# Hybrid attention layer on one core: the first norm's gain moved from x into the input weights, x loaded in half tiles

## The chip, the cores and the metric

The kernel runs on one core of a Trainium2 chip. The metric is the device time of one execution in microseconds; of several executions the median is given.

## The reference, cut to what matters

One decoder layer in float32 over 512 positions of width 1024. x is normalised and multiplied by a gain per feature, and one input projection of 1976 columns feeds both attention groups; output projection, second norm and a squared-ReLU MLP follow.

```python
def rms_norm(x, g):
    y = xf * lax.rsqrt(jnp.mean(xf * xf, axis=-1, keepdims=True) + EPS)
    return (y * g.astype(jnp.float32)).astype(x.dtype)

h = rms_norm(x, ln1_g) @ w_in      # columns: cq 384, ckv 256 + kr 32, nq 512, nsa k/v 768, gates 24
```

Since the gain stands on the contracted feature, (x * g) @ W equals x @ (g * W). The kernel leaves the factor per position, rsqrt of the mean square, until the results are read out of PSUM.

## The kernel before, in words

**Products in three parts.** Each float32 operand is split into a rounded high part (fp32r, written by ACT, the scalar engine) and the low remainder (written by DVE, the vector engine). PE (the tensor engine) forms a product as high times high, high times low and low times high (`three`, L2105 to L2110).

**Pieces of weights.** `PIECES` lists the weights in the order in which they are used, as pieces of up to 128x1024 values. Pieces 0 to 3 are block "cq" (768 columns: two feature chunks of 384), 4 to 7 "ckv" (576), then come uq, nq, ukv, nkv, cmp and others. Of the input projection's blocks (`IN_BLOCKS`) there are 20 pieces, four of each block. SP, the queue of SyncE, loads piece n into one of three `raw` buffers (L727), and must first wait for the low half of piece n-3 (`raw_free`). `split_hi` (ACT, L955 to L966) and `split_lo` (DVE, L1383 to L1394) turn it into the two halves in a ring of five. In between SP issues what `TURNED_AT`, `ROWS_AT` and `COPIES` name for a piece: the transposed tiles of x ahead of pieces 0, 2 and 3, the four row tiles of x ahead of piece 4, `gain_c` after piece 4, the constants after piece 6.

**x.** It is loaded twice: by rows (`x`, for the squares in `ln1_square`, L986) and features-first, four tiles of 128 positions (`x_t`). Tile 0 comes together with the gain of the norm (`x_first`); ACT and DVE multiply the gain in while they split it, in eight steps of 128 columns (`first_his` L992, `first_lows` L1414). Tiles 1 to 3 are multiplied by the gain on POOL, six operations of 128x512 (L774), and then split by `ln1_his` (L1000) and `ln1_lows` (L1424).

**The order of the head** is written out by hand for each engine. PE runs three warm-up matmuls of 512 columns in plain float32 (two passes each, L2210), then `latent_part("cq", i, t)`: for each tile t the pieces 0, 1, 2, then piece 3 for all tiles, then "ckv" piece by piece over the tiles. Both blocks of tile t use the same PSUM bank (`latent_bank(t)`), so that ckv of tile t waits for the copy of cq:

```python
if name == "ckv" and i == 0:
    pe.wait_ge(*copied.at(("cq", t)))
```

ACT's queue in the head is: splits of x and pieces 0 to 3, two squares, piece 4, two squares, and then

```python
for m in (5, 6, 7):
    split_hi(SPLITS[m])
for t in range(NT):
    cq_out(t)
```

where `cq_out` (L1027, L1028) squares the bank and copies it to `c_row`. POOL computes the reciprocal roots for both (L778, L763, L766). The later pieces of the input projection are split between other work: nq and nkv beside the expansion of the latents, the last ones beside the first attention units; DVE's low halves stand in one queue with head sums, row scalings and the first half of each softmax (L1565).

Of the kernel before, what the change touches and what calls it, by code (L numbers as in the profile page):

```python
# [22 lines left out]
ALU = mybir.AluOpType  # L23
# [98 lines left out]
TURNED_AT, ROWS_AT = {0: (0,), 2: (1,), 3: (2, 3)}, {4: (0, 1, 2, 3)}  # L122
# [203 lines left out]
def build(nc, a, out, known):  # L326
    with ExitStack() as ctx:
# [66 lines left out]
        x_first = place("x_first", KD + D_MODEL, at=r_mk + 24576)  # L394
        gain1 = x_first[:, 0:KD]
        x_t = [x_first[:, KD:].rearrange("p (k s) -> p k s", k=KD)] + [x_later[:, t, :, :] for t in range(NT - 1)]
# [121 lines left out]

        ident = const("ident")
# [16 lines left out]
        neg_rs = stat(NT)  # L536
# [7 lines left out]
        xt_in = [signal(f"xt_in{t}", 16) for t in range(NT)]  # L544
# [3 lines left out]
        consts_in, gainc_in = signal("consts_in", 16), signal("gainc_in", 16)  # L548
# [96 lines left out]
        def latent_bank(t):  # L645
            return (S + O)[t]
# [42 lines left out]

        block = ctx.enter_context(nc.Block())  # L690
# [3 lines left out]
        def _(sp):  # L694
# [3 lines left out]
            def load_turned(t):  # L698
                if t == 0:
                    sp.dma_start(x_first, a["x_first"]).then_inc(*xt_in[0].mark())  # L700
                else:
                    sp.dma_start(x_t[t], a["x_t"][t - 1].rearrange("p (k s) -> p k s", k=KD)).then_inc(*xt_in[t].mark())

            for n, (what, i, width, split) in enumerate(PIECES):
                for t in TURNED_AT.get(n, ()):
                    load_turned(t)
# [20 lines left out]
                sp.dma_start(raw[:, n % RAW, 0:width], source).then_inc(*raw_in[n % RAW].mark(n))  # L727
# [27 lines left out]
        def _(pool):  # L755
# [193 lines left out]
        def _(act):  # L949
            act.dma_start(ident, a["consts"][:, 0:P]).then_inc(*ident_in.mark())  # L950

            def split_hi(n):

                width, hi = PIECES[n][2], halves_of(n)[0]
                act.wait_ge(*raw_in[n % RAW].at(n))  # L955
                if n == APART:
                    act.wait_ge(*mix_done.at((0, NT - 1)))
                elif SPLIT_AT[n] >= RING:
                    act.wait_ge(*used_by(SPLITS[SPLIT_AT[n] - RING]))
                if PIECES[n][0] == "wo":  # L960
# [27 lines left out]
            def first_his(ks):  # L988

                act.wait_ge(*xt_in[0].at())  # L990
                for k in ks:
                    ins = act.activation(act_hi[:, k, 0:P], x_t[0][:, k, :], ACT.Copy, scale=gain1[:, k:k + 1])  # L992
                    if k % 2:
                        ins.then_inc(*turn_hi.mark(("ln1", 0, k // 2)))

            def ln1_his(t):

                for half in range(2):
                    act.wait_ge(*pool_step.at(("xg", t, half)))
                    act.activation(act_hi[:, 4 * half:4 * half + 4, t * P:(t + 1) * P], x_t[t][:, 4 * half:4 * half + 4, :],  # L1000
                                   ACT.Copy).then_inc(*turn_hi.mark(("ln1", t, half)))
# [380 lines left out]
        def _(dve):  # L1382
            def split_lo(n):  # L1383

                width, (hi, lo) = PIECES[n][2], halves_of(n)
                dve.wait_ge(*hi_done.at(n))
                if PIECES[n][0] == "wo":
                    for j, gain in enumerate(group_gains(n)):
                        cols = slice(512 * j, 512 * j + 512)
                        ins = dve.scalar_tensor_tensor(lo[:, cols], raw[:, n % RAW, cols], gain,  # L1390
                                                       hi[:, cols].bitcast(F32), ALU.mult, ALU.subtract)
                else:
                    ins = dve.tensor_tensor(lo[:, 0:width], raw[:, n % RAW, 0:width],  # L1393
                                            hi[:, 0:width].bitcast(F32), ALU.subtract)  # L1394
                ins.then_inc(*lo_done.mark(n))
# [13 lines left out]
            def first_lows(ks):  # L1409

                for k in ks:
                    if k % 2 == 0:
                        dve.wait_ge(*turn_hi.at(("ln1", 0, k // 2)))
                    ins = dve.scalar_tensor_tensor(act_lo[:, k, 0:P], x_t[0][:, k, :], gain1[:, k:k + 1],  # L1414
                                                   act_hi[:, k, 0:P].bitcast(F32), ALU.mult, ALU.subtract)
                    if k % 2:
                        ins.then_inc(*turn_lo.mark(("ln1", 0, k // 2)))

            def ln1_lows(t):

                for half in range(2):
                    ks, cols = slice(4 * half, 4 * half + 4), slice(t * P, (t + 1) * P)
                    dve.wait_ge(*turn_hi.at(("ln1", t, half)))
                    dve.tensor_tensor(act_lo[:, ks, cols], x_t[t][:, ks, :], act_hi[:, ks, cols].bitcast(F32),  # L1424
                                      ALU.subtract).then_inc(*turn_lo.mark(("ln1", t, half)))
# [664 lines left out]
        def _(pe):  # L2090
# [86 lines left out]
            def latent_part(name, i, t):  # L2177
# [3 lines left out]
                pe.wait_ge(*turn_lo.at(("ln1", t, i // 2 if t else i)))  # L2181
# [498 lines left out]
```

## Time and profile before

| what | us |
|---|---|
| median of 3 runs | 645.41 (645.12 to 646.32) |
| span of the profiled execution | 643.3 |
| time of the profiled execution | not listed apart; the median is 2.1 above the span |
| PE busy | 632.1 (98%) |
| DVE, ACT, POOL busy | 497.3, 399.1, 171.9 |

The span reaches from the first to the last instruction. PE, PEld, DVE, ACT, POOL and SPq (SyncE's queue) are the rows of the engines; a time in square brackets is idle time of the engine before the instruction, with what ended it. PEclk is the granted clock of TensorE, DMA share and GB/s are those of the core's 16 DMA engines. Matmuls are pipelined, so a long busy share of PE does not mean that it runs at its peak.

### The profile page before, as it was taken

What the parts mean: (1) busy time and instruction counts of PE and PEld (TensorE: products, weight loads), DVE (VectorE), ACT (ScalarE), POOL (GpSimd) and SP (SyncE); (2) the same over time, 40 slices, a digit from 0 to 9 for tenths busy, and PEclk for the clock granted to TensorE, in tenths of its full rate; (3) what the DMA queues carried; (4) which work ended last, traced back from release to release, by engine and by line L of the source; (5) the groups of instructions that cost most, each with busy time, mean ns of one, the idle gap of its engine ahead of it and who ended that gap; (6) DMA issues with size and microseconds to landing.
All of it is one profiled execution on the core that took longest, in us unless ns stands there. A gap on an engine that the chain in (4) does not pass through costs nothing.

```text
span 643.3 us, 11728 instructions
## 1 busy us (share of the span) xinstructions
PE 632.1 (98%) x4153; PEld 560.3 (87%) x4153; DVE 497.3 (77%) x913; ACT 399.1 (62%) x791; POOL 171.9 (27%) x236
## 2 busy tenths in 40 slices
PE   7999999999999999999999999999999999999998
PEld 4999788887789888887999999999998788888886
DVE  6665766589887878897885787777768999897676
ACT  6864675567897647657447666756647555664561
POOL 5656656434412202212110011110111221222200
DMA  9871729998988955995372687788877899999984
GB/s 337 311 268 71 261 72 356 290 292 207 263 255 274 343 178 173 286 288 106 67 198 99 170 230 213 195 230 196 214 179 168 201 245 224 225 239 269 261 258 150
DMA packets 34507, 142.50 MB, mean 222 GB/s; under 512 B 5159, under 2 KB 5543, under 8 KB 33488
## 3 DMA queue, kind: packets, MB, share of 16 engines
q1 hardware_dynamic: 22688, 83.72, 37.4%
q0 software_dynamic: 10208, 34.88, 29.8%
q10 hardware_dynamic: 1552, 23.14, 9.6%
q8 instruction: 34, 0.56, 0.3%
q14 instruction: 25, 0.20, 0.1%
HBM read 139.57 MB, written 65.06 MB: 318 GB/s over the span
## 4 chain that ended last, share of the span: by engine, by line
PE 91%; DVE 4%; ACT 2%; issue 1%; DMA 1%; SPq 0%; ACTq 0%; DVEq 0%
PE bank L2108 15%; PE bank L2109 15%; PE bank L2110 15%; PE bank L2502 7%; PE bank L2504 7%; PE bank L2503 7%; PE bank L2128 7%; PE bank L2337 3%; PE bank L2280 2%; PE bank L2319 2%; PE bank L2434 2%; PE bank L2433 2%; PE bank L2432 2%; PE bank L2291 1%; PE bank L2292 1%
## 5 line engine op out<-in xcount | busy, mean ns | idle before, releaser
L868 POOL DMA_DIRECT2D down_sums<-w_down x64 | 50.0, 781 | 235.0 <-PE bank L2504 143.0
L1393 DVE TENSOR_TENSOR w_lo<-raw,w_hi 128x1024 fp32r<-128x1024 f32 (+3 forms) x70 | 80.9, 1169 | 26.5 <-ACT w_hi L965 26.1
L2108 PE MATMUL bank<-w_hi,act_hi 128*128 128x512 f32 (+3 forms) x224 | 89.2, 398 | 3.2 <-DVE w_lo L1393 3.0
L965 ACT ACTIVATE w_hi<-raw 128x1024 fp32r<-128x1024 f32 (+3 forms) x70 | 68.1, 991 | 34.1 <-DMA raw<-w_pairs 27.3
L2109 PE MATMUL bank<-w_lo,act_hi 128*128 128x512 f32 (+3 forms) x224 | 79.7, 356 | 0.0
L2110 PE MATMUL bank<-w_hi,act_lo 128*128 128x512 f32 (+3 forms) x224 | 79.7, 356 | 0.0
L1119 ACT ACTIVATE p_buf<-s_buf,stats 128x128 f32<-128x128 f32 (+3 forms) x96 | 53.8, 561 | 32.4 <-PE bank L2128 17.3
L1354 ACT ACTIVATE w_hi<-raw 128x1024 fp32r<-128x1024 f32 x31 | 32.8, 1058 | 35.7 <-DMA raw<-down_sums 18.1
L2108 PE MATMUL bank<-w_hi,s_all 128*128 128x512 f32 x140 | 54.6, 390 | 0.0
L2109 PE MATMUL bank<-w_lo,s_all 128*128 128x512 f32 x140 | 54.5, 389 | 0.0
L2110 PE MATMUL bank<-w_hi,s_all 128*128 128x512 f32 x140 | 54.5, 389 | 0.0
L2108 PEld LDWEIGHTS bank<-w_hi,act_hi 128*128 128x128 f32 x224 | 42.1, 188 | 12.7 <-issue 5.3
L2502 PE MATMUL bank<-g_all,w_hi 128*128 128x256 f32 x168 | 47.6, 283 | 0.0
L2504 PE MATMUL bank<-act_hi,w_lo 128*128 128x256 f32 x168 | 47.5, 283 | 0.0
L2503 PE MATMUL bank<-act_lo,w_hi 128*128 128x256 f32 x168 | 47.5, 283 | 0.0
L2504 PE MATMUL bank<-g_all,w_lo 128*128 128x256 f32 x168 | 47.5, 283 | 0.0
L2503 PE MATMUL bank<-g_all,w_hi 128*128 128x256 f32 x168 | 47.5, 283 | 0.0
L2502 PE MATMUL bank<-act_hi,w_hi 128*128 128x256 f32 x168 | 47.5, 283 | 0.0
L2109 PEld LDWEIGHTS bank<-w_lo,act_hi 128*128 128x128 f32 x224 | 42.3, 189 | 5.9 <-issue 1.2
L2110 PEld LDWEIGHTS bank<-w_hi,act_lo 128*128 128x128 f32 x224 | 42.1, 188 | 5.4
L1991 DVE TENSOR_TENSOR w_lo<-raw,w_hi 128x1024 fp32r<-128x1024 f32 x31 | 37.8, 1220 | 10.5 <-ACT w_hi L1354 10.5
L2128 PE MATMUL bank<-consts,p_buf 128*128 128x128 f32 x248 | 45.0, 279 | 1.0 <-ACT m_k L1068 0.3
(317 smaller groups left out, 1833.6 us busy)
## 6 DMA issues: line engine op xcount, KB each, us to landing
down_sums<-w_down ACTq DMA_DIRECT2D x32, 512.0 KB, 6.3
down_sums<-w_down POOLq DMA_DIRECT2D x64, 256.0 KB, 5.9
raw<-down_sums SPq DMA_DIRECT2D x32, 512.0 KB, 5.3
up_sums<-w_pairs POOLq DMA_DIRECT2D x28, 512.0 KB, 9.8
raw<-up_sums SPq DMA_DIRECT2D x28, 512.0 KB, 4.8
raw<-weights SPq DMA_DIRECT2D x26, 512.0 KB, 5.7
up_sums<-w_pairs SPq DMA_DIRECT2D x16, 512.0 KB, 6.6
raw<-w_down SPq DMA_DIRECT2D x16, 512.0 KB, 5.3
```

What stands on the lines that cost most here:

```text
L868: pool.dma_start(sums_dram[k, rows_], a["w_down"][SUMS[m][1], step, rows_], accum_op=ALU.add, max_dma_last_dim=4096).then_inc(*sum_added[k ...
L965: ins = act.activation(hi[:, 0:width], raw[:, n % RAW, 0:width], ACT.Copy)
L1119: act.activation(p_buf[:, n % 2, 0:nk], s_buf[:, n % 2, 0:nk], ACT.Exp, scale=-1.0, bias=neg_max[:, m:m + 1], accum_out=den[:, d:d + 1]).t ...
L1393: ins = dve.tensor_tensor(lo[:, 0:width], raw[:, n % RAW, 0:width], hi[:, 0:width].bitcast(F32), ALU.subtract)
L1991: dve.tensor_tensor(lo, src, hi.bitcast(F32), ALU.subtract).then_inc(*lo_done.mark(JOBS[d]))
L2108: pe.matmul(dst, a_h, w_h, start=start, stop=False, skip_group_check=onto)
L2109: pe.matmul(dst, a_h, w_l, start=False, stop=False, skip_group_check=onto)
L2110: return pe.matmul(dst, a_l, w_h, start=False, stop=stop, skip_group_check=onto)
L2128: ins = pe.transpose(bank[0:m, i * step:i * step + k], tile, ident[0:k, 0:k])
L2502: pe.matmul(dst, h[:, k * P:(k + 1) * P], g_h[:, k, :], start=start and k == 0, stop=False, skip_group_check=onto)
L2503: pe.matmul(dst, h[:, k * P:(k + 1) * P], g_l[:, k, :], start=False, stop=False, skip_group_check=onto)
L2504: ins = pe.matmul(dst, l[:, k * P:(k + 1) * P], g_h[:, k, :], start=False, stop=k == KD // 2 - 1, skip_group_check=onto)
```

## The change

The gain is no longer multiplied into x. `split_hi` and `split_lo` of the 20 pieces of the input projection multiply it into the weights, as two halves of a piece, one for each feature chunk; DVE can begin when the first half of the high part is there. POOL's six operations go. x features-first comes in eight half tiles of 256 KB, each split when it has landed; SP issues the first halves ahead of pieces 0 and 2, the second halves ahead of pieces 3 and 4, and two of the row tiles ahead of piece 5 instead of 4. Piece 0 and the gain (32 bytes per partition, a tile of its own) are issued by ACT, ahead of the identity. PE takes pieces 0 and 1 for each tile, then piece 2 over all tiles, then piece 3; the third warm-up matmul has 256 columns instead of 512. On DVE the order is the same as ACT's (`ln1_low` in place of `first_lows` and `ln1_lows`), and the host passes `x_t` whole and the gain as an array of its own.

```diff
--- before.py
+++ after.py
-TURNED_AT, ROWS_AT = {0: (0,), 2: (1,), 3: (2, 3)}, {4: (0, 1, 2, 3)}
+TURNED_AT = {0: [(0, 0)], 2: [(1, 0), (2, 0), (3, 0)], 3: [(0, 1)], 4: [(1, 1), (2, 1), (3, 1)]}
+ROWS_AT = {4: (0, 1), 5: (2, 3)}
...
-        x_first = place("x_first", KD + D_MODEL, at=r_mk + 24576)
-        gain1 = x_first[:, 0:KD]
+        x_first = place("x_first", D_MODEL, at=r_mk + 24576).rearrange("p (k s) -> p k s", k=KD)
...
+        def norm_gains(n):
+            k = 2 * PIECES[n][1]
+            return [gain1[:, j:j + 1] for j in (k, k + 1)]
...
-            def load_turned(t):
-                if t == 0:
-                    sp.dma_start(x_first, a["x_first"]).then_inc(*xt_in[0].mark())
-                else:
-                    sp.dma_start(x_t[t], a["x_t"][t - 1].rearrange("p (k s) -> p k s", k=KD)).then_inc(*xt_in[t].mark())
+            def load_turned(t, half):
+                ks = slice(4 * half, 4 * half + 4)
+                sp.dma_start(x_t[t][:, ks, :], a["x_t"][t].rearrange("p (k s) -> p k s", k=KD)[:, ks, :]).then_inc(*xt_in[t][half].mark())
...
-                sp.dma_start(raw[:, n % RAW, 0:width], source).then_inc(*raw_in[n % RAW].mark(n))
+                if n:
+                    sp.dma_start(raw[:, n % RAW, 0:width], source).then_inc(*raw_in[n % RAW].mark(n))
...
-            pool.wait_ge(*xt_in[0].at())
-            for t in range(1, NT):
-                pool.wait_ge(*xt_in[t].at())
-                for half in range(2):
-                    rows_ = x_t[t][:, 4 * half:4 * half + 4, :]
-                    pool.tensor_tensor(rows_, rows_, gain1[:, 4 * half:4 * half + 4].unsqueeze(2).to_broadcast([P, 4, P]),
-                                       ALU.mult).then_inc(*pool_step.mark(("xg", t, half)))
...
         def _(act):
+            act.dma_start(raw[:, 0, 0:PIECES[0][2]], a["weights"][0, :, 0:PIECES[0][2]]).then_inc(*first_piece_in)
+            act.dma_start(gain1, a["ln1_g"]).then_inc(*gain1_in.mark())
             act.dma_start(ident, a["consts"][:, 0:P]).then_inc(*ident_in.mark())
...
+                elif PIECES[n][0] in IN_BLOCKS:
+                    if n == 0:
+                        act.wait_ge(*gain1_in.at())
+                    for j, gain in enumerate(norm_gains(n)):
+                        cols = slice(j * width // 2, (j + 1) * width // 2)
+                        ins = act.activation(hi[:, cols], raw[:, n % RAW, cols], ACT.Copy, scale=gain)
+                        if j == 0:
+                            ins.then_inc(*hi_done.mark((n, 0)))
...
-            def first_his(ks):
...
-            def ln1_his(t):
...
+            def ln1_hi(t, half):
+                act.wait_ge(*xt_in[t][half].at())
+                act.activation(act_hi[:, 4 * half:4 * half + 4, t * P:(t + 1) * P], x_t[t][:, 4 * half:4 * half + 4, :],
+                               ACT.Copy).then_inc(*turn_hi.mark(("ln1", t, half)))
...
-            first_his(range(4))
+            ln1_hi(0, 0)
             split_hi(SPLITS[0])
-            first_his(range(4, KD))
             split_hi(SPLITS[1])
+            for t in range(1, NT):
+                ln1_hi(t, 0)
             split_hi(SPLITS[2])
-            ln1_his(1)
-            ln1_his(2)
+            ln1_hi(0, 1)
             split_hi(SPLITS[3])
-            ln1_his(3)
+            for t in range(1, NT):
+                ln1_hi(t, 1)
             ln1_square(0)
             ln1_square(1)
             split_hi(SPLITS[4])
...
             def split_lo(n):
-                dve.wait_ge(*hi_done.at(n))
+                dve.wait_ge(*hi_done.at((n, 0) if PIECES[n][0] in IN_BLOCKS else n))
...
+                elif PIECES[n][0] in IN_BLOCKS:
+                    for j, gain in enumerate(norm_gains(n)):
+                        cols = slice(j * width // 2, (j + 1) * width // 2)
+                        if j:
+                            dve.wait_ge(*hi_done.at(n))
+                        ins = dve.scalar_tensor_tensor(lo[:, cols], raw[:, n % RAW, cols], gain,
+                                                       hi[:, cols].bitcast(F32), ALU.mult, ALU.subtract)
...
-                pe.wait_ge(*turn_lo.at(("ln1", t, i // 2 if t else i)))
+                pe.wait_ge(*turn_lo.at(("ln1", t, i // 2)))
...
-            for _ in range(3):
-                pe.matmul(latent_bank(NT - 1), warm[:, 0:P], warm, start=True, stop=True)
+            for n in (512, 512, 256):
+                pe.matmul(latent_bank(NT - 1)[:, 0:n], warm[:, 0:P], warm[:, 0:n], start=True, stop=True)
             for t in range(NT):
-                for i in range(3):
+                for i in range(2):
                     latent_part("cq", i, t)
-            for t in range(NT):
-                latent_part("cq", 3, t)
+            for i in (2, 3):
+                for t in range(NT):
+                    latent_part("cq", i, t)
```

## Rows read from the trace of the kernel before

**Rows 1.** The page, part 1: busy time of the engines

```profile
PE 632.1 (98%) x4153; PEld 560.3 (87%) x4153; DVE 497.3 (77%) x913; ACT 399.1 (62%) x791; POOL 171.9 (27%) x236
```

**Rows 2.** Waits of PE, whole span (total us, times, longest us)

```profile
PE bank L2108 <- DVE w_lo L1393: 3.0, 4, 1.4
```

**Rows 3.** PE in order of time, 0 to 30 us (start us, length us)

```profile
1.44 5.49 PE L2210 MATMUL bank<-warm 128*128 128x512 f32 x6 [1.44 <-DVE warm L1442]
...
7.61 0.41 PE L2108 MATMUL bank<-w_hi,act_hi 128*128 128x384 f32 x1 [0.68 <-DVE w_lo L1393]
...
9.53 0.41 PE L2108 MATMUL bank<-w_hi,act_hi 128*128 128x384 f32 x1 [0.61 <-DVE w_lo L1393]
...
12.24 0.41 PE L2108 MATMUL bank<-w_hi,act_hi 128*128 128x384 f32 x1 [1.43 <-DVE w_lo L1393]
...
27.08 0.33 PE L2110 MATMUL bank<-w_hi,act_lo 128*128 128x384 f32 x1
27.25 0.29 PE L2108 MATMUL bank<-w_hi,act_hi 128*128 128x288 f32 x1
...
29.64 0.30 PE L2108 MATMUL bank<-w_hi,act_hi 128*128 128x288 f32 x1
```

**Rows 4.** ACT in order of time, 4 to 29 us and at 136 us

```profile
4.46 1.28 ACT L992 ACTIVATE act_hi<-x_first 128x128 fp32r<-128x128 f32 x4 [1.79 <-DMA x_first<-x_first]
...
5.64 0.83 ACT L965 ACTIVATE w_hi<-raw 128x768 fp32r<-128x768 f32 x1
...
24.60 0.69 ACT L965 ACTIVATE w_hi<-raw 128x576 fp32r<-128x576 f32 x1 [0.29 <-DMA raw<-weights]
25.19 0.56 ACT L1027 ACTIVATE square<-bank,stats 128x384 f32<-128x384 f32 x1
...
28.80 0.62 ACT L1028 ACTIVATE c_row<-bank,stats 128x384 f32<-128x384 f32 x1
...
136.42 1.32 ACT L963 ACTIVATE w_hi<-raw,consts 128x512 fp32r<-128x512 f32 x2
```

**Rows 5.** POOL and DVE in order of time, 8 to 19 us

```profile
8.56 5.88 POOL L774 TENSOR_TENSOR x_t<-x_t,x_first 128x512 f32<-128x512 f32 x4 [6.55 <-DMA x_t<-x_t]
...
10.35 1.75 DVE L1393 TENSOR_TENSOR w_lo<-raw,w_hi 128x768 fp32r<-128x768 f32 x1 [0.97 <-ACT w_hi L965]
...
17.81 0.95 DVE L1393 TENSOR_TENSOR w_lo<-raw,w_hi 128x768 fp32r<-128x768 f32 x1
```

**Rows 6.** Stretches of the head (PE, PEld, DVE, ACT, POOL busy; clock; DMA share, GB/s)

```profile
13.00:17.00 4.00, 3.95 (x23) 3.62 (x22) 4.00 (x4) 2.63 (x4) 4.00 (x3) 1.00 1.03 414
17.00:19.00 2.00, 2.00 (x14) 2.00 (x13) 2.00 (x3) 1.63 (x3) 0.34 (x1) 1.00 1.03 391
19.00:23.00 4.00, 4.00 (x25) 4.00 (x24) 1.72 (x3) 3.82 (x8) 1.77 (x3) 1.00 0.87 308
```

**Rows 7.** SyncE's queue in order of time: pieces 6 and 7

```profile
18.79 0.33 SPq L727 DMA_DIRECT2D raw<-weights  x1
...
21.69 3.86 SPq L727 DMA_DIRECT2D raw<-weights  x3
```

**Rows 8.** DMA issue at 21.69, piece 7 (KB, us to landing)

```profile
raw<-weights SPq DMA_DIRECT2D x1, 288.0 KB, 2.9
```

**Rows 9.** Lines L1390 and L1393, DVE's low halves (ns, shortest/median/longest)

```profile
L1390 DVE SCALAR_TENSOR_TENSOR w_lo<-raw,consts,w_hi x16: 745/747/1185, 138.3 to 262.9; 128x512 fp32r<-128x512 f32 x16
...
L1393 DVE TENSOR_TENSOR w_lo<-raw,w_hi x70: 733/1225/1749, 6.5 to 475.5; 128x1024 fp32r<-128x1024 f32 x55, 128x768 fp32r<-128x768 f32 x7, 128x576 fp32r<-128x576 f32 x4, 128x560 fp32r<-128x560 f32 x4
```

**Rows 10.** DVE and PE in order of time, 70 to 100 us

```profile
70.29 2.88 DVE L1393 TENSOR_TENSOR w_lo<-raw,w_hi 128x1024 fp32r<-128x1024 f32 x2
...
71.83 0.50 PE L2108 MATMUL bank<-w_hi,act_hi 128*128 128x512 f32 x1 [0.26 <-DVE w_lo L1393]
...
97.64 1.49 DVE L1393 TENSOR_TENSOR w_lo<-raw,w_hi 128x1024 fp32r<-128x1024 f32 x1
...
99.19 0.53 PE L2108 MATMUL bank<-w_hi,act_hi 128*128 128x512 f32 x1
```

More of the change, by code:

```diff
@@ L393, in build @@
         x_later = place("x_t", (NT - 1) * D_MODEL, at=r_work).rearrange("p (t k s) -> p t k s", t=NT - 1, k=KD)
-        x_first = place("x_first", KD + D_MODEL, at=r_mk + 24576)
-        gain1 = x_first[:, 0:KD]
-        x_t = [x_first[:, KD:].rearrange("p (k s) -> p k s", k=KD)] + [x_later[:, t, :, :] for t in range(NT - 1)]
+        x_first = place("x_first", D_MODEL, at=r_mk + 24576).rearrange("p (k s) -> p k s", k=KD)
+        x_t = [x_first] + [x_later[:, t, :, :] for t in range(NT - 1)]
         ln_sq = place("ln_sq", D_MODEL + 1, at=r_mk + 16384)
@@ L535, in build @@
         pe_col, pe_lo, kc_ss, kc_rs = stat(2), stat(2), stat(1), stat(1)
-        neg_rs = stat(NT)
+        neg_rs, gain1 = stat(NT), stat(KD)
         banks = [psum(f"bank{i}") for i in range(8)]
@@ L543, in build @@
         x_in = [signal(f"x_in{t}", 16) for t in range(NT)]
-        xt_in = [signal(f"xt_in{t}", 16) for t in range(NT)]
+        xt_in = [[signal(f"xt_in{t}{half}", 16) for half in range(2)] for t in range(NT)]
         x_back, x_rest = signal("x_back", 16), signal("x_rest", 16)
@@ L547, in build @@
         ident_in = signal("ident_in", 16)
-        consts_in, gainc_in = signal("consts_in", 16), signal("gainc_in", 16)
+        consts_in, gainc_in, gain1_in = signal("consts_in", 16), signal("gainc_in", 16), signal("gain1_in", 16)
         onehot_in, vec_out = signal("onehot_in", 16), signal("vec_out", 16)
@@ L688, in copy_quadrants @@
                 engine.dma_start(sums_dram[k], a["w_down"][SUMS[m][0], step]).then_inc(*sum_copied[k // 8].mark(k))
+        first_piece_in = raw_in[0].mark(0)
         block = ctx.enter_context(nc.Block())
@@ L696, in load_x @@
                 sp.dma_start(x[:, t, :], a["x"][t * P:(t + 1) * P, :]).then_inc(*x_in[t].mark())
-            def load_turned(t):
-                if t == 0:
-                    sp.dma_start(x_first, a["x_first"]).then_inc(*xt_in[0].mark())
-                else:
-                    sp.dma_start(x_t[t], a["x_t"][t - 1].rearrange("p (k s) -> p k s", k=KD)).then_inc(*xt_in[t].mark())
+            def load_turned(t, half):
+                ks = slice(4 * half, 4 * half + 4)
+                sp.dma_start(x_t[t][:, ks, :], a["x_t"][t].rearrange("p (k s) -> p k s", k=KD)[:, ks, :]).then_inc(*xt_in[t][half].mark())
             for n, (what, i, width, split) in enumerate(PIECES):
-                for t in TURNED_AT.get(n, ()):
-                    load_turned(t)
+                for t, half in TURNED_AT.get(n, ()):
+                    load_turned(t, half)
                 for t in ROWS_AT.get(n, ()):
@@ L1407, in to_lo, with ln1_low @@
                 dve.tensor_tensor(dst, src, hi.bitcast(F32), ALU.subtract).then_inc(*turn_lo.mark(key))
[L1409 to L1425, printed above, removed]
+            def ln1_low(t, half):
+                ks, cols = slice(4 * half, 4 * half + 4), slice(t * P, (t + 1) * P)
+                dve.wait_ge(*turn_hi.at(("ln1", t, half)))
+                dve.tensor_tensor(act_lo[:, ks, cols], x_t[t][:, ks, :], act_hi[:, ks, cols].bitcast(F32),
+                                  ALU.subtract).then_inc(*turn_lo.mark(("ln1", t, half)))
             def ln2_rows(t, cols=slice(0, D_MODEL)):
@@ L1442, in _ @@
             dve.memset(warm, 1.0).then_inc(*dve_step.mark("warm"))
-            first_lows(range(4))
+            ln1_low(0, 0)
             split_lo(SPLITS[0])
-            first_lows(range(4, KD))
             split_lo(SPLITS[1])
+            for t in range(1, NT):
+                ln1_low(t, 0)
             split_lo(SPLITS[2])
-            ln1_lows(1)
-            ln1_lows(2)
+            ln1_low(0, 1)
             split_lo(SPLITS[3])
-            ln1_lows(3)
+            for t in range(1, NT):
+                ln1_low(t, 1)
             split_lo(SPLITS[4])
@@ L2665 @@
     arrays = {
-        "x": v["x"][0], "x_t": x_t[1:], "x_first": np.concatenate([v["ln1_g"].reshape(KD, P).T, x_t[0]], axis=1), "weights": weights, "w_down": down, "w_pairs": pairs, "consts": consts, "onehot": onehot, "rel_bias": v["rel_bias"],
+        "x": v["x"][0], "x_t": x_t, "ln1_g": v["ln1_g"].reshape(KD, P).T, "weights": weights, "w_down": down, "w_pairs": pairs, "consts": consts, "onehot": onehot, "rel_bias": v["rel_bias"],
         "gain_c": rows(v["mla_cq_norm_g"], v["mla_ckv_norm_g"]),
```

9 lines of the change are left out of this document (removed).

## The prediction

> **What bounds the kernel now.** The page's first part comes first: TensorE is busy for 98% of the span [rows 1], so only its idle time and its own work can change the time much. The waits of PE over the whole span come next: its largest entry is 3.0 us in four waits for DVE's low halves of the weights [rows 2], and PE in order of time puts three of them in the head. The warm-up ends at 6.93 (1.44 + 5.49); the first product starts at 7.61 after 0.68 idle, then come stops of 0.61 before 9.53 and 1.43 before 12.24; a little later PE runs dense, a 384-column matmul every 0.17 us (27.08 to 27.25), and reaches the block "ckv" at 27.25 [rows 3]. The "cq" block is 96 such matmuls, 16.6 us at 0.173, and takes 19.6 from 7.61: 3.0 us of holes are what the change can reach. The question is what comes due just behind, so the third view is ACT in order of time. ACT's queue has three splits (pieces 5, 6 and 7) ahead of the read-out of the four cq banks. The last of them, at 24.60, has waited 0.29 for its transfer; the read-out then runs from 25.19 to 29.42 (28.80 + 0.62) [rows 4]. PE's ckv matmuls for tile t reuse bank t and wait for that copy: tile 3 starts at 29.64 [rows 3]. PE usually follows a release by about 0.15 us (DVE's low half of piece 2 ends at 12.10, PE starts on it at 12.24 [rows 5, 3]). So tile 3 has 29.64 - 29.42 - 0.15 = 0.07 us of slack: the read-out chain already lies level with PE.
>
> **The parts of the change.**
> - *Head of PE.* ACT begins now when x_first lands, at 4.46 [rows 4]. After the change it waits for a half tile (256 KB instead of 516); piece 0 goes out on a second queue; and the small gain row becomes a new condition of ACT's first split. The operations up to the end of piece 0 about balance: one 128x512 copy and two gained halves for four 128-column copies and one 768-column split, likewise on DVE. No row shows when the gain row lands: at the least together with piece 0, at the most 2.2 us behind it, which is what piece 7's landing of 2.9 us holds beyond its 288 KB at 391 GB/s [rows 6, 8]. I put PE's first product at 7.5, bounds 6.8 to 8.4. After that ACT and DVE take about 1 us for each piece and 0.6 for each half tile; PE uses 1.04 us for each pair of piece and tile. In the new order piece 2 is wanted only after eight such pairs, near 15.9. So the stops before 9.53 and 12.24 go, and cq ends near 7.5 + 16.6 + 0.1 = 24.2 instead of 27.25: **3.0 us earned**.
> - *POOL's six gain multiplications* go (the first four take 5.88 us from 8.56). PE does not wait for POOL itself, but DVE is stretched beside it: a 768-column low half takes 1.75 us there and 0.95 alone [rows 5]. This is part of the same 3.0 us.
> - *The warm-up* loses one sixth, 0.9 us, and ends near 6.0; PE then idles 1.5 us instead of 0.68. The granted clock reads 1.00 in every stretch [rows 6]. If the first products ran at the lower level all the same (1.2 instead of 2.4 GHz), ten of them would cost 10 x 0.17 = 1.7 us; the 2.6 us of waiting found in the next points cover it.
> - *What is late next: piece 7 and the read-out.* PE wants ckv at 24.2, but ACT must first split piece 7, which is issued at 21.69 and lands 2.9 later, at 24.59 [rows 7, 8]. The bytes ahead of it are the same before and after. What differs is a hole: SP issues piece 6 only when DVE has finished the low half of piece 3 (17.81 + 0.95; issue at 18.79 [rows 5, 7]), and the DMA engines run low meanwhile, 308 GB/s in the four microseconds from 19, against 391 and 414 before [rows 6]. At 400 that is 4 x 92 = 368 KB, 0.9 us. With piece 3 split near 12.5, piece 6 and the constants join the queue in time and the hole closes. Against it, 2 MB of x come in rows of 2 KB instead of 4: the stretch with much of the narrower weight rows moves 391 GB/s instead of 414 [rows 6], 6%, so 5 us of transfer grow by 0.3. Piece 7 then lands 0.6 earlier, near 24.0. Bounds: 1.3 earlier (two queues fill the first microseconds better) and 0 (the hole opens elsewhere).
> - *Its split* is two gained halves. Two 512-column ones take 1.32 us; 768 against 576 columns (0.83 and 0.69) give 0.73 ns per column, so two of 288 take 1.32 - 448 x 0.00073 = 0.99, and the next instruction starts 0.10 before that end, as at 25.19: 0.89 instead of 0.59 [rows 4], 0.3 back. The read-out starts 0.6 - 0.3 = 0.3 earlier; with the slack of 0.07 PE gains **0.4 us** at tile 3 of ckv. The other 2.6 of the 3.0 turn into waits for ACT before 29.3.
> - *Twelve later pieces* (four each of nq, nkv, cmp) get the same dearer split. On DVE two halves are 2 x 0.745 less an overlap of 0.08, 1.41 against 1.22: +0.19 each [rows 9]. At two places PE already meets a low half. At 71.83 it has waited 0.26 for the first of two that fill DVE from 70.29 for 2.88 us; the second ends at 73.17, just ahead of its use. At 99.19 PE starts on a piece whose low half ran from 97.64 to 99.13 [rows 10]. First place 2 x 0.19 less 0.1, second 0.2. Bounds: 0 (DVE may start after half of a split) and 12 x 0.19 = 2.3, if all showed. I take **0.5 back**, since PE's list shows no other wait for w_lo [rows 2].
>
> Sum: -0.4 + 0.5 = +0.1. For DVE's earlier start I take 0.2 off. The profiled execution has a span of 643.3 and I add the 2.1 around it, which makes it equal to the median, 645.41; the forecast is **645.3**.
>
> **Rivals.**
> (A) The 3.0 us pass through. The read-out would have to start by 22.6, so piece 7 land by 21.7; for it speaks only that the byte count alone allows a better use of the first microseconds. 645.4 - 3.0 + 0.5 = 642.9. Chance 0.12.
> (B) The DMA hole only moves: SP now has its x transfers behind two waits for low halves, and issues piece 3 or 4 into an empty queue. Piece 7 lands at 24.6; PE pays 0.3 and 0.5, less the slack: 646.1. Chance 0.15.
> (C) Slower, in the stretch from 64 to 132 us: DVE's chain to PE. If all twelve dearer low halves fall on it, 2.3 back less 0.4 gained: 647.3. It decides from nine visible ones (1.7). Against it: only two places show it now. Chance 0.10.
> (D) Each transfer brings a fixed time in the queue: the 2.2 us of piece 7's landing beyond its bytes. Five more transfers go ahead of piece 7: 11 us, 656. Against it: 414 GB/s through transfers of 384 and 512 KB [rows 6], which leaves no room between them. Chance 0.01.
> The Trainium skill, "DMA: Bandwidth & Descriptors", section on bandwidth, asks for transfers of 1 MiB and more and gives a fixed price of about 2.0 us each; by that rule halving the tiles is the wrong way, and the sum would be about 10 us worse. The trace shows such a time at the landing of a lone transfer and not between queued ones.
>
> **How the numbers follow.** The forecast has 0.62, A 0.12, B 0.15, C 0.10, D 0.01. The forecast's own range is 644.3 to 646.3, from the bounds of the landing and a give-back of 0 to 1. The range 643.8 to 646.6 takes in B and leaves out A, D and most of C. A measurement of this kernel tells about 0.2%, 1.3 us: faster is below 644.1, slower above 646.7. Faster: A and the forecast's edge, 0.18. Slower: most of C, and D, 0.10. The same: 0.72.
>
> **What would show it.** Right: PE dense from its first product to about 24.2; then a wait of about 1.3 us for ACT's c_row at the first ckv matmul and shorter ones at tiles 1 to 3, tile 3 starting near 29.2; piece 7 landing near 24.0; no multiplications on POOL; PE's waits for w_lo near 71 and 99 longer by 0.2 to 0.3. Wrong: ckv's tile 3 before 28.3 (A); a DMA share below 0.9 between 9 and 20 us (B); PE's waits for DVE from 64 to 132 us longer by 1.5 (C); a first product after 9.

## The result, and the profile after

| | before | changed |
|---|---|---|
| median (20 runs each) | 645.41 us | 648.57 us (647.87 to 651.73) |
| span of the profiled execution | 643.3 | 646.9 |
| ratio | | 1.0038, 95% interval 1.0026 to 1.0051 |

The change makes the kernel slower, by 3.2 us in the median and by 1.7 to 3.3 going by the interval. The forecast was 645.3 within 643.8 to 646.6: wrong in size and in sign. The page's first part and the waits of PE over the whole span, of the changed kernel (total us, times, longest us), answer to [rows 1, 2]:

```profile
PE 631.6 (98%) x4153; PEld 560.6 (87%) x4153; DVE 496.1 (77%) x927; ACT 404.3 (62%) x805; POOL 159.8 (25%) x230
```

```profile
PE bank L2106 <- ACT c_row L1029: 3.4, 1, 3.4
PE bank L2106 <- DVE w_lo L1398: 3.3, 3, 2.3
```

Busy times hardly moved. One wait of 3.4 us for ACT, which was not there before, now leads. PE in order of time, changed kernel (answers to [rows 3]):

```profile
1.44 4.63 PE L2208 MATMUL bank<-warm 128*128 128x512 f32 x6 [1.44 <-DVE warm L1439]
8.35 0.41 PE L2106 MATMUL bank<-w_hi,act_hi 128*128 128x384 f32 x1 [2.27 <-DVE w_lo L1398]
...
24.92 0.34 PE L2108 MATMUL bank<-w_hi,act_lo 128*128 128x384 f32 x1
28.68 0.37 PE L2106 MATMUL bank<-w_hi,act_hi 128*128 128x288 f32 x1 [3.43 <-ACT c_row L1029]
...
31.64 0.37 PE L2106 MATMUL bank<-w_hi,act_hi 128*128 128x288 f32 x1
```

The block "cq" is dense, 96 matmuls from 8.35 to 25.1, and ends 2.2 us earlier than before. But tile 3 of "ckv" starts at 31.64 instead of 29.64. So the gain was real and was turned into a wait. In the kernel before, ckv ran on from cq without one (27.08, 27.25 [rows 3]); now the read-out ends two microseconds later, and PE follows it. ACT in order of time shows what it waited for itself (answers to [rows 4]; L970 is the gained high part, L995 a square, L1028 and L1029 the read-out):

```profile
4.88 0.63 ACT L1000 ACTIVATE act_hi<-x_first 128x512 fp32r<-128x512 f32 x1 [1.24 <-DMA x_first<-x_t]
6.41 2.13 ACT L970 ACTIVATE w_hi<-raw,stats 128x384 fp32r<-128x384 f32 x4 [0.90 <-DMA stats<-ln_g]
...
13.85 1.12 ACT L970 ACTIVATE w_hi<-raw,stats 128x384 fp32r<-128x384 f32 x2 [2.20 <-DMA raw<-weights]
...
21.24 1.07 ACT L995 ACTIVATE ln_sq<-x 128x1025 f32<-128x1025 f32 x1 [0.85 <-DMA x<-x]
...
26.45 0.96 ACT L970 ACTIVATE w_hi<-raw,stats 128x288 fp32r<-128x288 f32 x2 [1.06 <-DMA raw<-weights]
27.31 0.56 ACT L1028 ACTIVATE square<-bank,stats 128x384 f32<-128x384 f32 x1
```

Every wait from 13.85 on is for a transfer. The last, piece 7, is split at 26.45 (24.60 before), so the read-out of cq starts at 27.31 instead of 25.19. SyncE's queue of the changed kernel (L733 is a piece, L707 half tiles of x) and the issue of piece 7 (KB, us to landing; answers to [rows 7, 8]):

```profile
8.23 0.33 SPq L733 DMA_DIRECT2D raw<-weights  x1
8.60 1.38 SPq L707 DMA_DIRECT2D x_t<-x_t  x3
...
20.97 5.33 SPq L733 DMA_DIRECT2D raw<-weights  x3
```

```profile
raw<-weights SPq DMA_DIRECT2D x1, 288.0 KB, 5.5
```

Piece 7 is issued 0.7 us earlier than before and lands 1.9 later, because a backlog stands ahead of it. Where the backlog comes from is seen in the same four stretches of both kernels (PE, PEld, DVE, ACT, POOL busy; clock; DMA share, GB/s). Before:

```profile
8.00:12.00 4.00, 2.20 (x12) 1.57 (x10) 3.03 (x4) 2.49 (x4) 3.44 (x3) 1.00 1.02 405
12.00:16.00 4.00, 3.70 (x20) 3.40 (x21) 4.00 (x4) 2.07 (x4) 4.00 (x4) 1.00 1.04 420
16.00:20.00 4.00, 4.00 (x25) 4.00 (x25) 3.96 (x5) 3.10 (x5) 2.01 (x2) 1.00 0.94 352
20.00:24.00 4.00, 4.00 (x25) 4.00 (x24) 0.99 (x2) 3.91 (x9) 1.77 (x4) 1.00 0.86 313
```

Changed:

```profile
8.00:12.00 4.00, 3.65 (x21) 3.61 (x22) 4.00 (x8) 3.65 (x8) 0.00 (x0) 1.00 0.84 297
12.00:16.00 4.00, 4.00 (x25) 4.00 (x24) 2.23 (x5) 2.15 (x5) 0.00 (x0) 1.00 0.91 322
16.00:20.00 4.00, 4.00 (x25) 4.00 (x24) 1.46 (x4) 3.31 (x8) 0.95 (x2) 1.00 1.04 416
20.00:24.00 4.00, 4.00 (x25) 4.00 (x24) 0.94 (x2) 3.02 (x6) 0.96 (x3) 1.00 1.03 401
```

The hole of before, after 16 us, is closed, as forecast. A larger one has opened at 8 to 16: (405 + 420 - 297 - 322) x 4 = 824 KB fewer are moved there. SP issues piece 3 only when the low half of piece 0 has freed its buffer, here at 8.2. Before, 516 KB of tile 0 and three tiles of 512 KB were issued ahead of that wait. After, five half tiles of 256 KB are, and three half tiles stand behind it: 772 KB less in the queue. All that is issued ahead of the wait, on all queues, comes to 2500 KB (2.56 MB), and that is what the DMA engines have moved by 9.5 us (269 GB/s from 0 to 9.5): the queue runs dry. The missing bytes are not the whole of the hole, though:

```profile
11.00:12.00 1.00, 1.00 (x8) 1.00 (x7) 1.00 (x3) 0.65 (x2) 0.00 (x0) 1.00 0.61 178
12.00:13.00 1.00, 1.00 (x8) 1.00 (x7) 0.73 (x2) 0.00 (x0) 0.00 (x0) 1.00 0.69 170
```

In these two microseconds piece 3 and the three half tiles have long been issued (from 8.23 to 9.55) and none of them has landed. So after it has run dry the queue also comes back slowly: the reason stays open, and that 772 and 824 KB lie so close proves little.

Where the loss builds up is best seen by comparing the start of the same matmul in two traces, counted back from the last one. Each line is worked out in this way from one profiled execution (us against before; negative is earlier; the columns are times of the kernel before). The execution can be off its kernel's median: those of e1 and e8 are the slowest of theirs, those of e3 and e10 the fastest.

| kernel | 25 | 45 | 80 | 110 | 550 |
|---|---|---|---|---|---|
| changed | -2.16 | +2.07 | +2.85 | +3.23 | +3.42 |
| halves ahead (e1) | -0.66 | -0.49 | +0.29 | +0.66 | +1.51 |
| gain row first (e2) | -0.61 | +1.42 | +2.21 | +2.59 | +2.75 |
| late pieces plain (e3) | -0.65 | +1.23 | +1.22 | +1.22 | +1.20 |
| read-out first (e4) | +0.37 | +0.37 | +1.09 | +1.49 | +1.71 |
| e1 and e4 (e5) | -0.77 | -0.77 | -0.04 | +0.38 | +0.93 |
| e5, longer warm-up (e6) | -2.09 | -2.07 | -1.32 | -0.93 | -0.59 |
| e5, other order of low halves (e7) | -0.58 | -0.58 | +7.00 | +7.40 | +7.61 |
| whole tiles (e8) | -0.19 | -0.03 | +0.69 | +1.03 | +1.21 |
| longer warm-up alone (e9) | -2.04 | +2.26 | +3.04 | +3.41 | +3.76 |
| e6, late pieces plain (e10) | -2.18 | -2.18 | -2.17 | -2.19 | -2.19 |
| before, read-out first (e11) | +0.04 | +0.04 | +0.06 | 0.00 | +0.01 |

So the head gives +2.07 of the changed kernel's loss, 71 to 80 us +0.78, the rest +0.57. For the 0.78, DVE and PE of the changed kernel near 71 and 99 us (answers to [rows 10]):

```profile
72.38 3.63 DVE L1398 SCALAR_TENSOR_TENSOR w_lo<-raw,stats,w_hi 128x512 fp32r<-128x512 f32 x4
...
100.47 1.82 DVE L1398 SCALAR_TENSOR_TENSOR w_lo<-raw,stats,w_hi 128x512 fp32r<-128x512 f32 x2
```

```profile
74.25 0.50 PE L2106 MATMUL bank<-w_hi,act_hi 128*128 128x512 f32 x1 [0.60 <-DVE w_lo L1398]
```

Two low halves took 2.88 us together and now take 3.63; the one near 99 took 1.49 and takes 1.82. PE waits 0.60 where it waited 0.26 and is held up once more by the second piece.

### The profile page after: what moved, and what is told of

Same layout as the page of the kernel before. It is cut to its first block, busy times and chain, and to the rows that moved or that the text cites. A ratio compares the mean times of both kernels' runs of the same rounds, so it can differ in the third digit from the quotient of the medians.

```text
span 646.9 us, 11756 instructions
## 1 busy us (share of the span) xinstructions
PE 631.6 (98%) x4153; PEld 560.6 (87%) x4153; DVE 496.1 (77%) x927; ACT 404.3 (62%) x805; POOL 159.8 (25%) x230
## 4 chain that ended last, share of the span: by engine, by line
PE 87%; DVE 4%; ACT 2%; issue 2%; ACTq 0%; DVEq 0%
PE bank L2106 14%; PE bank L2108 14%; PE bank L2107 14%; PE bank L2501 7%; PE bank L2503 7%; PE bank L2502 7%; PE bank L2126 6%; PE bank L2336 3%; PE bank L2279 2%; PE bank L2318 2%; PE bank L2431 2%; PE bank L2433 2%; PE bank L2432 2%; PE bank L2290 1%; PE bank L2291 1%
## 5 line engine op out<-in xcount | busy, mean ns | idle before, releaser
L1401 DVE TENSOR_TENSOR w_lo<-raw,w_hi 128x1024 fp32r<-128x1024 f32 (+1 forms) x50 | 59.8, 1209 | 17.2 <-ACT w_hi L974 16.8
L974 ACT ACTIVATE w_hi<-raw 128x1024 fp32r<-128x1024 f32 (+1 forms) x50 | 51.4, 1040 | 28.3 <-DMA raw<-w_pairs 25.9
```

## The experiments

Beside each group of experiments the kernel before was run again. It had 645.49 us beside e1 to e4 (35 runs), 645.32 beside e5 to e8 (27) and 646.30 beside e9 to e11 (23), so the ratios compare better than the times. Their intervals are some 0.3% wide; the table above separates causes more finely, but from one execution each.

**e1: the second halves of x ahead of the wait.**

```diff
-TURNED_AT = {0: [(0, 0)], 2: [(1, 0), (2, 0), (3, 0)], 3: [(0, 1)], 4: [(1, 1), (2, 1), (3, 1)]}
+TURNED_AT = {0: [(0, 0)], 2: [(1, 0), (2, 0), (3, 0)], 3: [(0, 1), (1, 1), (2, 1), (3, 1)]}
```

> Edit to the changed kernel: the three second half tiles go out ahead of piece 3, before SyncE's wait for the low half of piece 0. Theory 1 (late issue: behind that wait, at 8.2 us, the queue has nothing left, moves 271, 336, 178 and 170 GB/s in the microseconds from 9 to 13, and piece 7 and the read-out of cq come late): the hole closes to under 0.5 us, piece 7 lands near 24.6 instead of 26.5, tile 3 of ckv starts 1.9 us earlier, time 646.7. Theory 2 (rows of 2 KB are slow in themselves): the low rates only move, time within 0.4 of 648.6.

646.51 us, ratio 1.0011 [0.9996, 1.0026]. Stretches of the head, and ACT at piece 7:

```profile
8.00:12.00 4.00, 3.73 (x15) 3.70 (x16) 4.00 (x9) 3.56 (x7) 0.00 (x0) 0.72 1.04 403
12.00:16.00 4.00, 4.00 (x21) 4.00 (x21) 2.77 (x6) 2.77 (x6) 0.00 (x0) 0.86 1.03 404
```

```profile
23.89 0.96 ACT L970 ACTIVATE w_hi<-raw,stats 128x288 fp32r<-128x288 f32 x2 [0.84 <-DMA raw<-weights]
```

With nothing but this order changed the hole is gone (403 and 404 GB/s), piece 7 is split 2.56 us earlier, and 2.56 of the head's loss goes; the median falls by 2.06. The order of issue against the wait is the cause. The granted clock in this execution was 0.50 from 10 to 12 us, so that cq ended 1.5 later than in the changed kernel (-0.66 against -2.16 in the table); the later read-out hid that. A further 0.7 us, lost at 144 us in this execution, appears in e5 in part (0.4) and in no other; it was not followed up.

**e2: the gain row ahead of piece 0 on ACT's queue.**

```diff
+            act.dma_start(gain1, a["ln1_g"]).then_inc(*gain1_in.mark())
             act.dma_start(raw[:, 0, 0:PIECES[0][2]], a["weights"][0, :, 0:PIECES[0][2]]).then_inc(*first_piece_in)
-            act.dma_start(gain1, a["ln1_g"]).then_inc(*gain1_in.mark())
```

> Edit to the changed kernel: ScalarE issues the gain row before piece 0 instead of behind it. Theory 1 with the gain row as its trigger (it lands at 6.3, 1.2 us after piece 0 at 5.1): low half of piece 0 done near 7.3 instead of 8.2, piece 3 issued 0.9 earlier, the hole from 9 to 13 shorter by about 0.9, time 647.7. If the gain row is not what holds the first split, or the hole does not depend on when piece 3 is issued: PE's first product moves but the time stays within 0.3 of 648.6.

648.33 us, ratio 1.0039 [1.0024, 1.0054]: nothing gained. ACT of this kernel:

```profile
6.54 2.13 ACT L970 ACTIVATE w_hi<-raw,stats 128x384 fp32r<-128x384 f32 x4 [2.05 <-DMA raw<-weights]
```

The gain row is in time now, but piece 0 lands at 6.5 instead of 5.1, so the split starts at 6.54 against 6.41. Of the 1.4 us, 0.45 is the later issue. The rest is not the price of the small row: in the changed kernel the row and SP's piece 1, both issued at 1.17, take the same time to land,

```profile
raw<-weights SPq DMA_DIRECT2D x1, 384.0 KB, 5.0
stats<-ln_g ACTq DMA_DIRECT2D x1, 4.0 KB, 5.1
```

and in e2 it is piece 0 that is issued at 1.18, beside the same piece 1, and takes 5.3. What is issued first on its queue, at 0.73, took 4.4 (piece 0) in the changed kernel and 3.3 (the row) here. Going by these landings, the two queues share the DMA engines, and whatever ACT issues second lands with SP's second.

**e3: the gain left out of the twelve later pieces** (nq, nkv and cmp are split as before; their results lack the gain).

```diff
+GAINED = ("cq", "ckv")
-                elif PIECES[n][0] in IN_BLOCKS:
+                elif PIECES[n][0] in GAINED:
```

> Edit to the changed kernel: only the eight pieces of cq and ckv are multiplied by the gain; the twelve of nq, nkv and cmp are split plainly, as before (so the first norm's gain is left out of these blocks). Theory 3 (the dearer splits lengthen DVE's queue where PE waits for it: PE loses 0.8 us between 71 and 80 and 0.3 near 100): both losses go, time 647.4, the first 32 us unchanged. Rival (these losses come from transfers or from the shifted head): they stay, 648.5.

647.94 us, ratio 1.0033 [1.0020, 1.0046]. DVE and PE near 71 us:

```profile
71.52 2.88 DVE L1402 TENSOR_TENSOR w_lo<-raw,w_hi 128x1024 fp32r<-128x1024 f32 x2
```

```profile
73.05 0.50 PE L2107 MATMUL bank<-w_hi,act_hi 128*128 128x512 f32 x1 [0.25 <-DVE w_lo L1402]
```

The rows are those of before again, and from 45 us on this execution loses nothing (+1.23 to +1.20). The dearer splits cost 3.42 - 2.07 = 1.35 us, the forecast had 0.5. The median fell by only 0.6. This head gave +1.23, not +2.07, and behind PE's last matmul the execution loses 0.9 (span +2.1 against +1.20), so the parts don't add up to the median better than to a microsecond.

**e4: the read-out of cq ahead of piece 7's split**, in ACT's and, alike, in DVE's queue.

```diff
-            for m in (5, 6, 7):
+            for m in (5, 6):
                 split_hi(SPLITS[m])
             for t in range(NT):
                 cq_out(t)
+            split_hi(SPLITS[7])
```

> Edit to the changed kernel: ScalarE reads out the four cq banks before it splits piece 7, and DVE scales them before the low half of piece 7. Theory 4 (the read-out is late only because it stands behind piece 7's transfer): it starts when piece 6 is split, near 25.4 instead of 27.3, tile 3 of ckv 1.9 earlier, time 646.7. Rival (something else holds it, the squares' chain or PE's later need of piece 7): under 0.5 gained, a wait of PE for the low half of piece 7 shows instead.

646.73 us, ratio 1.0009 [0.9996, 1.0022]. ACT and PE:

```profile
25.51 0.56 ACT L1028 ACTIVATE square<-bank,stats 128x384 f32<-128x384 f32 x1
```

```profile
8.32 0.66 PE L2108 MATMUL bank<-w_hi,act_hi 128*128 128x384 f32 x1 [2.24 <-DVE w_lo L1399]
8.77 0.52 PE L2109 MATMUL bank<-w_lo,act_hi 128*128 128x384 f32 x1
...
27.62 0.29 PE L2108 MATMUL bank<-w_hi,act_hi 128*128 128x288 f32 x1
```

The hole is still there (308 and 283 GB/s from 8 to 16 us), and yet the read-out starts 1.80 earlier and the median falls by 1.84: the late transfer did its harm through its place in ACT's queue, ahead of work that did not need it. That this execution shows no wait for c_row has a second cause, and it is luck. Its first seventeen products start 0.32 us apart, to 13.6 us, instead of 0.17, so ckv can start at 27.62 and not at 25.1. From 25.1 a wait of some 1.5 us would be left, by an estimate from the rows (the copy of tile 0 ends at 26.6). The spacing of 0.32 is that of e1 at a granted clock of 0.50. The clock column reads 1.00 here all the same: this trace has no clock record before 13.87, and an interval without one is shown as 1.00.

**e5: e1 and e4 together.**

```diff
-TURNED_AT = {..., 3: [(0, 1)], 4: [(1, 1), (2, 1), (3, 1)]}
+TURNED_AT = {..., 3: [(0, 1), (1, 1), (2, 1), (3, 1)]}
-            for m in (5, 6, 7):
+            for m in (5, 6):
...
+            split_hi(SPLITS[7])
```

> Edit to the changed kernel: both edits of e1 and e4 (second half tiles ahead of piece 3; read-out of cq ahead of piece 7). If the transfers and the queue order are the two causes of the loss in the head: the read-out starts when pieces 5 and 6 are split, near 23.1, PE's first ckv products at about 25 without a wait, 2.2 us earlier than in the kernel before; the 1.35 lost after 70 us stay: time 644.7. If they are one cause counted twice: 646.4, as either alone.

646.26 us, ratio 1.0022 [1.0009, 1.0036]: 1.6 above the 644.7 expected, and in number at the rival's 646.4. PE, and two microseconds of it:

```profile
1.45 4.02 PE L2210 MATMUL bank<-warm 128*128 128x512 f32 x6 [1.45 <-DVE warm L1440]
8.25 0.66 PE L2108 MATMUL bank<-w_hi,act_hi 128*128 128x384 f32 x1 [2.79 <-DVE w_lo L1399]
```

```profile
8.00:10.00 2.00, 1.75 (x6) 1.78 (x7) 2.00 (x5) 2.00 (x5) 0.00 (x0) 0.53 1.04 403
```

The warm-up ends at 5.5, PE idles 2.79 us, and its first products run at a granted clock of 0.53, near the lower level of 1.2 GHz. No wait for c_row covers this any more, so cq's own end sets the time. That is not the rival's mechanism, and e6 tells them apart. The twelve executions agree in part: one is at 644.69, six at 646.1 to 646.3 with a mean granted clock of 0.997, and five at 647.1 to 649.8 with a mean of 1.00. A mean of 1.00 is also what e4's slow-starting execution has, so the five may be like it; no trace of them was kept.

**e6: e5 with a warm-up of four matmuls of 512 columns.**

```diff
-            for n in (512, 512, 256):
+            for n in (512, 512, 512, 512):
```

> Edit to e5: the warm-up has four matmuls of 512 columns instead of 512, 512 and 256 (ends near 8.5, at the time of the first product, instead of 6.1). e1, e2 and e3 showed a granted clock of 0.57 to 0.72 from 8 to 12 us and their cq part ran 1.0 to 1.6 us late. Theory 5 (the shorter warm-up and the longer idle after it let the clock fall in some executions): clock 1.00 from 8 to 12, and, since in e5 nothing hides that part, a time up to 1.0 below e5's, with less spread. Rival (the clock is not set by this): same clock pattern, same time within 0.2.

**644.82 us** (644.48 to 645.25, 11 runs), ratio 0.9987 [0.9974, 1.0000]. PE, ACT and the clock:

```profile
1.45 5.90 PE L2210 MATMUL bank<-warm 128*128 128x512 f32 x8 [1.45 <-DVE warm L1440]
8.41 0.41 PE L2108 MATMUL bank<-w_hi,act_hi 128*128 128x384 f32 x1 [1.07 <-DVE w_lo L1399]
...
25.17 0.29 PE L2108 MATMUL bank<-w_hi,act_hi 128*128 128x288 f32 x1
```

```profile
23.20 0.56 ACT L1028 ACTIVATE square<-bank,stats 128x384 f32<-128x384 f32 x1
```

```profile
8.00:12.00 4.00, 3.59 (x21) 3.55 (x22) 4.00 (x8) 3.70 (x8) 0.00 (x0) 1.00 1.04 401
```

The first product starts no earlier than in e5, but at full clock; "ckv" starts at 25.17, 2.08 before its old place, and no wait for c_row is left. The median falls by 1.44 against e5, more than the 1.0 allowed for, and all eleven executions have a mean clock of 1.00. Of the versions that compute all of it this is the fastest, and it has the narrowest spread, but its advantage of 0.5 to 0.6 us is at the edge of what these runs resolve.

**e7: e5 with the low half of piece 14 after those of 15 and 16.**

```diff
-ROW_LOWS, UNIT_LOWS = {**ROW_SPLITS, 7: (18,)}
+ROW_LOWS, UNIT_LOWS = {**ROW_SPLITS, 3: (13, 15, 16, 14), 7: (18,)}
```

> Edit to e5: DVE forms the low halves of pieces 13 to 16 in the order 13, 15, 16, 14 instead of 13, 14, 15, 16, since PE wants 15 and 16 first. Theory 3 (the loss of 0.8 between 71 and 80 us is DVE's queue of dearer low halves): 0.4 of it goes, as piece 15 is ready at 70 and piece 16 is then bound by its transfer; time 0.4 below e5. Rival: piece 14 or piece 17 comes late instead and eats it, same time.

653.07 us, ratio 1.0119 [1.0106, 1.0132]: a plain miss. ACT and DVE:

```profile
70.06 1.33 ACT L970 ACTIVATE w_hi<-raw,stats 128x512 fp32r<-128x512 f32 x2 [2.42 <-DMA raw<-weights]
```

```profile
72.74 1.21 DVE L1402 TENSOR_TENSOR w_lo<-raw,w_hi 128x1024 fp32r<-128x1024 f32 x1
```

```profile
PE bank L2108 <- DVE w_lo L1402: 5.1, 1, 5.1
```

Of the 7.6 us lost between 45 and 80, the wait is 5.1; behind it, from 75 to 80 us, the granted clock was 0.50. Piece 16 could not be had that early, since its transfer waits for a freed raw buffer; piece 14, which PE wanted first, stood behind it on DVE. It is the same error as the change makes in the head: needed work queued behind a late transfer.

**e8: tiles 1 to 3 whole, in rows of 4 KB, ahead of piece 2**; tile 0 in halves ahead of pieces 0 and 3.

```diff
-TURNED_AT = {0: [(0, 0)], 2: [(1, 0), (2, 0), (3, 0)], 3: [(0, 1)], 4: [(1, 1), (2, 1), (3, 1)]}
+TURNED_AT = {0: [(0, 0)], 2: [(1, 0), (2, 0), (3, 0)], 3: [(0, 1)]}
-                ks = slice(4 * half, 4 * half + 4)
+                ks = slice(4 * half, 4 * half + 4) if t == 0 else slice(0, KD)
```

> Edit to the changed kernel: tiles 1 to 3 of x features-first come whole, in rows of 4 KB, ahead of piece 2; only tile 0 comes in halves. The same bytes are ahead of SyncE's wait as in e1, with larger rows. Theory 1 (only the late issue matters): as e1, 646.5 within 0.3. Theory 2 (rows of 2 KB are slow): 0.5 or more faster than e1, and more than 404 GB/s from 8 to 16.

647.17 us, ratio 1.0022 [1.0013, 1.0032]; 404 and 392 GB/s in 8 to 16 us. Fewer and wider transfers are no faster than e1's halves (403 and 404): neither the 2 KB rows nor the number of transfers is the cause. The time is outside the 646.5 within 0.3 of theory 1 as well: piece 7 is split at 24.35 here, 0.46 behind e1.

**e9: the changed kernel with e6's warm-up alone.**

```diff
-            for n in (512, 512, 256):
+            for n in (512, 512, 512, 512):
```

> The changed kernel with a warm-up of four matmuls of 512 columns instead of 512, 512 and 256; nothing else. Theory 1: the clock only decides when cq ends, and in the changed kernel cq's end is hidden behind a 3.4 us wait for the read-out of cq, which hangs on piece 7's landing. So the median stays where it is: 648.4 +- 0.5, ratio to the kernel before 1.003 to 1.005. Rival: the cold first products are part of the changed kernel's 3.2 us, as they were in the version with both repairs; then it comes out 1 to 1.5 us lower, near 647.2.

649.69 us (6 runs), ratio 1.0063 [1.0045, 1.0081]. PE, and the stretch behind its wait:

```profile
27.91 0.42 PE L2106 MATMUL bank<-w_hi,act_hi 128*128 128x288 f32 x1 [2.54 <-ACT c_row L1029]
```

```profile
28.00:30.00 2.00, 2.00 (x9) 2.00 (x10) 1.07 (x2) 2.00 (x7) 1.63 (x4) 0.52 1.06 397
```

The rival (1 to 1.5 us gained) falls, and the time is above theory 1's 648.4 +- 0.5 too. With six executions its interval still overlaps that of the changed kernel, so that it is slower isn't shown. The head shift is that of the changed kernel (+2.26 against +2.07). Here the granted clock was 0.52 behind the idle time before ckv, which ate the 0.8 us by which this read-out began earlier (26.54 against 27.31). The same wait in the changed kernel, longer, left it at 1.00.

**e10: e6 with the later pieces plain** (the gain left out of nq, nkv and cmp, as in e3). On top of e6:

```diff
-                elif PIECES[n][0] in IN_BLOCKS:
+                elif PIECES[n][0] in GAINED:
```

> The second halves of x ahead of piece 3, the read-out of cq ahead of piece 7's split, the warm-up of 4 x 512, and the gain left out of nq, nkv and cmp (so these twelve pieces are split as in the kernel before; their results lack the gain). Theory 1: the head keeps its -2.4 us from 25 us on and nothing is given back later, so the shift stays at -2.4 to the end: 645.3 - 2.4 = 642.9, ratio 0.9965. Rival: the later loss is not the dearer splits but the earlier timing of everything behind the head against the DMA queue, and would come back in another form: 644.5 or more.

644.46 us, ratio 0.9982 [0.9965, 1.0000]. DVE near 71 us:

```profile
68.11 2.88 DVE L1403 TENSOR_TENSOR w_lo<-raw,w_hi 128x1024 fp32r<-128x1024 f32 x2
```

The head's -2.18 stays to the last matmul. Against e6's -0.59 that prices the dearer splits at 1.5 us once more. The span is shorter by 1.3 only: about 0.9 goes behind PE's last matmul, as in e3; there the last addition on DVE starts only after 0.46 us of idle time. The median expected was 642.9; four of the twelve runs lie near 647.3, the other eight between 643.91 and 644.77. So the shift bears out theory 1, but the median does not: 644.46 is at the rival's 644.5, and against the kernel before, run beside it (1.84 below), it falls between theory 1's 2.4 and the rival's 0.8.

**e11: the kernel before with e4's edit.**

```diff
-            for m in (5, 6, 7):
+            for m in (5, 6):
                 split_hi(SPLITS[m])
             for t in range(NT):
                 cq_out(t)
+            split_hi(SPLITS[7])
```

> The kernel before with one edit: the read-out of the four cq banks stands ahead of piece 7's split in ACT's and DVE's queues. Theory 1 (the prediction's reading: the read-out chain lies level with PE in the kernel before, with 0.07 us of slack, and PE's own cq end at 27.25 binds as well): nothing gained, 645.3 +- 0.4, ratio 0.999 to 1.001. Rival 1: the read-out was the bound there already, and starting it 0.6 us earlier gives 0.5 us: 644.8. Rival 2: piece 7's split, now behind four read-outs, comes too late for PE: 647 or more.

645.24 us, ratio 0.9994 [0.9977, 1.0011]; the shift is 0.06 or less from 20 us on. By the trace theory 1 holds: before the change PE's own cq set the time and the read-out only lay level with it. The ratio's interval alone would not exclude rival 1's 0.5 us.

## Why the prediction was wrong, point by point

- **PE's gain: right.** The first product came at 8.35 (7.5 forecast, bounds 6.8 to 8.4): the gain row landed 1.2 us behind piece 0, within the bounds given. From there cq was dense as worked out (16.7 us for 96 matmuls; 16.6 + 0.1 forecast) and ended at 25.1. 2.2 us were earned, not 3.0.
- **The step that failed: "The bytes ahead of it are the same before and after", "the hole closes", "Piece 7 then lands 0.6 earlier".** It counted bytes, and looked only at the later of SP's waits. It did not count how many of them are issued ahead of the first wait, the one before piece 3. That is 772 KB less, and 824 KB fewer were moved from 8 to 16 us. Piece 7 landed at 26.5 instead of 24.6. The bound "0 (the hole opens elsewhere)" was set as if a moved hole could be no larger than the old one. e1 is the proof: one line, 2.56 us back in the trace, 2.06 in the median.
- **Rival B** named just this mechanism, SP's x transfers behind waits for low halves, and its sign (DMA share below 0.9: 0.84 was seen). It was priced at 0.3 plus 0.5; the head alone cost 2.1. Its chance of 0.15 was too low, since the order of SP's queue could be written out beforehand.
- **The chain piece 7, split, read-out, ckv: right**, and it carried the loss. The split cost 0.86 to the next start (0.89 forecast), and PE followed it copy by copy. e4 shows that the chain was the bound (1.84 us in the median), e11 that it was not yet so before.
- **The later splits: mechanism and place right, size wrong**, 1.35 us instead of 0.5, with the first place at 0.78 (0.28 forecast) and the second at 0.35 (0.2). The term came from halves at 0.745 us each [rows 9] in a quiet stretch. Near 71 us two such pairs took 3.63, 0.91 for each half, against 2.88 for two whole ones: +0.38 per piece instead of +0.19. e3 and e10 remove it. Rival C, all of it and 2.3 us, did not come.
- **The clock: right that a wait can cover it.** In the changed kernel's profiled execution there was nothing to cover (products 0.17 us apart from the first); in those of e1, e2 and e3 cq ended 1.5 us later, and the read-out still set the time behind it. Its price, put at 1.7 us for ten products, measured 1.3 to 1.4 (e5 against e6: -0.77 against -2.09 at 25 us, 646.26 against 644.82 us). In e4's execution seventeen products were slow, and cq ended 2.5 us later.
- **Rivals A and D** fell. A needed piece 7 by 21.7. For D, e8 has three transfers fewer than e1 and is 0.7 slower. The Trainium skill, "DMA: Bandwidth & Descriptors", section "Anatomy of one DMA" (not the one on bandwidth, which the prediction names), gives a fixed cost of about 2.0 us for a DMA issued from GpSimd; by an estimate from that figure e8 would have beaten e1 by some 6 us. Between queued transfers, which here are issued by SyncE, the trace does not agree with that price.

What stays open: in some executions PE loses a further 1.5 to 1.8 us, between 599 and 620 us. It is in the traces of e1, e2, e8 and e9 and in none of the others. In e9 a wait of 0.9 us for a DVE low half stands there. The table ends ahead of it, but how much of it is in the medians isn't known; it widens their spread.

## What to carry to other kernels

When a change splits or reorders transfers, write out the issuing queue of both versions with its waits, and count the bytes in the queue ahead of each wait: the sum before the last landing says nothing about when it happens. Work that does not need a late transfer should stand ahead of the split that does, since in-order queues turn a late piece into a wait for everything behind it. Shortening a warm-up and delaying the first product are one decision, and a price per instruction should be taken from the stretch in which it will run.

## What the runs showed of the hardware that was not expected

- Size did not decide when a transfer at the start landed: of two issued at 1.17 us on two queues, 384 KB took 5.0 us and a row of 4 KB 5.1. With the row first (e2), the 384 KB on ACT's queue, issued at 1.18, took 5.3.
- A DMA queue that had run dry did not come back at once: 178 and 170 GB/s from 11 to 13 us in the changed kernel, while four transfers issued from 8.23 to 9.55 had not landed, against 406 and 410 in e1, where three more half tiles stood ahead of the wait.
- The granted clock after idle time was not the same from run to run: 2.27 us idle left it at 1.00 in the changed kernel, 2.79 gave 0.53 in e5; 3.43 us before ckv left it at 1.00 in the changed kernel and 2.54 gave 0.52 in e9. After 1.07 us (e6) it stayed at 1.00.
- A clock column of 1.00 is no proof of the full clock: in e4 it stands beside products 0.32 us apart, where the full clock gives 0.17. The spacing of the matmuls is the surer sign.
